# Attention in a two-block kernel: the three value pairs of a head in one burst behind its six score tiles, the sums of a head pair in the second head's burst

## What is computed

```
def _attend_dense(q, k, v):
    s = jnp.einsum('bqhd,bkhd->bhqk', q, k, preferred_element_type=jnp.float32) * (QK_DIM ** -0.5)
    pr = jax.nn.softmax(s, axis=-1).astype(v.dtype)
    return jnp.einsum('bhqk,bkhd->bqhd', pr, v)

def _merge(p, attn_o, four_o, w_o_attn, w_fourier, w_out):
    ga = jax.nn.sigmoid(p[..., OFF_GA:OFF_GB])
    gb = jax.nn.sigmoid(p[..., OFF_GB:N_IN])
    return (ga * (attn_o @ w_o_attn) + gb * (four_o @ w_fourier)) @ w_out
```

## Time and profile before

| what | us |
|---|---|
| median of 3 runs (1334.64 to 1336.63) | 1335.6 |
| span of the profiled execution | 1332.2 |
| TensorE busy in it | 1313.8 (99%) |
| the eight heads, from the first score product of head 0 to the first product of attn_o | 89.4 (278.26 to 367.64) |

### The profile page before, as it was taken

One profiled execution on the slowest core, in us unless ns is written; L12 is line 12 of the kernel. 1 busy time (PEld: TensorE's weight loads), 2 busy tenths in 40 slices (PEclk: granted clock), 3 DMA queues, 4 the chain that ended last, 5 costly groups with the idle time before them and its releaser, 6 DMA issues.

```text
span 1332.2 us, 15820 instructions
## 1 busy us (share of the span) xinstructions
PE 1313.8 (99%) x6366; PEld 966.9 (73%) x6366; DVE 690.1 (52%) x1261; ACT 461.6 (35%) x618; POOL 433.8 (33%) x136
## 2 busy tenths in 40 slices
PE   8999999999999899999999999999999999999998
PEld 6789888865587834343457788888888888888887
DVE  2465987757783733343356656612562551551553
ACT  4335223345621221121135571433341431431431
POOL 3143244247612000000015333444245344444440
PEclk9999999999999899999999999999999999999999
DMA  9521198201025799999983122222132223123101
GB/s 378 214 96 64 58 356 336 103 1 64 32 96 189 294 375 421 421 421 420 421 367 127 63 80 110 96 95 95 63 126 98 93 95 118 71 94 126 64 1 64
DMA packets 34501, 226.70 MB, mean 170 GB/s; under 512 B 4064, under 2 KB 4704, under 8 KB 8448
## 3 DMA queue, kind: packets, MB, share of 16 engines
q1 hardware_dynamic: 32992, 218.93, 42.9%
q0 software_dynamic: 1152, 4.19, 0.8%
q10 hardware_dynamic: 288, 2.62, 0.5%
HBM read 221.53 MB, written 4.19 MB: 169 GB/s over the span
## 4 chain that ended last, share of the span: by engine, by line
PE 94%; DVE 3%; DMA 1%; ACT 1%; SPq 0%; issue 0%; DVEq 0%; ACTq 0%
PE psum L961 24%; PE psum L963 23%; PE psum L962 23%; PE psum L1465 13%; DMA mod_in<-in_stream 1%; PE psum L1273 1%; PE psum L1239 1%; PE psum L1450 1%; PE psum L1453 1%; PE psum L1008 1%; PE psum L1537 1%; PE psum L1425 1%; PE psum L1674 1%; DVE rs L2381 1%; PE psum L1013 0%; DVE work L2512 0%
## 5 line engine op out<-in xcount | busy, mean ns | idle before, releaser
L895 POOL TENSOR_TENSOR w_lo<-raw,w_hi 128x2048 fp32r<-128x2048 f32 x79 | 365.3, 4627 | 589.9 <-ACT w_hi L1704 589.9
L961 PE MATMUL psum<-b_hi,w_hi 128*128 128x512 f32 x608 | 238.1, 392 | 0.1
L963 PE MATMUL psum<-b_hi,w_lo 128*128 128x512 f32 x608 | 236.7, 389 | 0.0
L962 PE MATMUL psum<-b_lo,w_hi 128*128 128x512 f32 x608 | 236.6, 389 | 0.0
L1704 ACT ACTIVATE w_hi<-raw 128x2048 fp32r<-128x2048 f32 x80 | 152.6, 1907 | 145.4 <-PE psum L963 101.9
L961 PEld LDWEIGHTS psum<-b_hi,w_hi 128*128 128x128 f32 x608 | 114.1, 188 | 30.6 <-issue 5.7
L963 PEld LDWEIGHTS psum<-b_hi,w_lo 128*128 128x128 f32 x608 | 114.1, 188 | 23.9
L962 PEld LDWEIGHTS psum<-b_lo,w_hi 128*128 128x128 f32 x608 | 114.2, 188 | 23.4
L1465 PE MATMUL psum<-ex_ring,xe 128*64 128x512 f32 x488 | 108.8, 595 | 0.9 <-ACT xe L1929 0.9
L2429 DVE TENSOR_TENSOR x<-psum,x 128x512 f32<-128x512 f32 x40 | 27.4, 691 | 124.3 <-PE psum L963 124.3
L961 PE MATMUL psum<-h_hi,w_hi 128*128 128x512 f32 (+1 forms) x208 | 84.7, 407 | 1.3 <-POOL w_lo L878 1.3
(11 more groups left out here) (419 smaller groups left out, 2290.9 us busy)
## 6 DMA issues: line engine op xcount, KB each, us to landing
raw<-in_stream SPq DMA_DIRECT2D x97, 1024.0 KB, 4.8
ex_ring<-in_stream SPq DMA_DIRECT2D x89, 1024.0 KB, 17.7
mod_in<-in_stream SPq DMA_DIRECT2D x8, 1024.0 KB, 21.0
ex_last<-in_stream SPq DMA_DIRECT2D x7, 1024.0 KB
x<-in_x SPq DMA_DIRECT2D x4, 512.0 KB, 6.0
x<-in_x ACTq DMA_DIRECT2D x1, 2048.0 KB, 7.4
xt<-h2t SPq DMA_DIRECT2D x8, 256.0 KB, 11.7
out<-y_out SPq DMA_DIRECT2D x8, 256.0 KB, 3.3
```

Source lines behind the costliest of these rows:

```text
L895: nc.gpsimd.tensor_tensor(w_lo[:, slot, :], raw[:, raw_slot, :], w_hi[:, slot, :].bitcast(F32), ALU.subtract).then_inc(w_lo_done, 1)
L961: mm(o, w[0], x[0], start=start, stop=False)
L962: mm(o, w[0], x[1], start=False, stop=False)
L963: return mm(o, w[1], x[0], start=False, stop=stop)
```

## The change

In the plan, `sums` moves from the third score tile of an even head to the end of an odd head, from bank 5 to bank 1, and stands ahead of `mx_row`. On TensorE the third value pair moves from behind score tile 2 of the next head to the end of its own head's burst, and `sums` of a head pair follows directly behind the value pairs of the second head. On ScalarE the output of a head is taken behind exponential 1 instead of 2, and `rs` behind `max_row` at the end of an odd head. VectorE and GpSimd keep their order.

```diff
@@ make_plan
             p.add("sT", h, k, by="act", bank=k % 3)
-            if k == 2 and h >= 2 and h % 2 == 0:
-                p.add("sums", h // 2 - 1, by="act", bank=5)
             if k >= 2 and h + 1 < H:
                 max_pair(h + 1, k - 2)
+        if h % 2 == 1:
+            p.add("sums", h // 2, by="act", bank=1)
         if h + 1 < H:
             p.add("mx_row", h + 1, by="act", bank=0)
         if h + 2 < H:
             head_t(h + 2)
-    p.add("sums", H // 2 - 1, by="act", bank=5)
@@ TensorE
-                    if k == 2 and h >= 1:
-                        pv_pair(h - 1, KT - 2)
-                        if h % 2 == 0:
-                            prob_sums(h // 2 - 1)
                     if k >= 2 and h + 1 < H:
                         max_pair(h + 1, k - 2)
-                pv_pair(h, 0)
-                pv_pair(h, 2)
+                for k in range(0, KT, 2):
+                    pv_pair(h, k)
+                if h % 2 == 1:
+                    prob_sums(h // 2)
                 if h + 1 < H:
                     max_row(h + 1)
                 if h + 2 < H:
                     head_t(h + 2)
-            pv_pair(H - 1, KT - 2)
-            prob_sums(H // 2 - 1)
@@ ScalarE
-                    if k == 2 and h >= 1:
+                    if k == 1 and h >= 1:
                         output(h - 1)
-                        if h % 2 == 0:
-                            output_sums(h // 2 - 1)
...
                 if h + 1 < H:
                     max_row(h + 1)
+                    if h % 2 == 1:
+                        output_sums(h // 2)
             output(H - 1)
             output_sums(H // 2 - 1)
```

## The result

| what | before | after |
|---|---|---|
| median in a joint measurement (8 runs each), us | 1335.8 | 1339.9 |
| ratio after to before, 95% interval | | 1.0032 [1.0021, 1.0044] |
| span of the profiled execution, us | 1332.2 | 1338.1 |
| to the first score product of head 0 | 278.26 | 279.29 |
| from there to the first attn_o product | 89.38 | 94.06 |

The changed kernel is slower by 0.32%, about 4.3 us. The prediction was 1338.7 us, slower, with 1336.6 to 1340.4 as its range. In the profiled execution the eight heads take 4.68 us more, where +3.15 was forecast. The 1.03 us before the first head arise in the first 47 us, where TensorE's listed waits for the input transfer `mod_in` (1.3 us for 0.8) and for ScalarE's squares of the input (2.3 for 0.7) are longer.

What follows compares the result with a forecast made beforehand. TensorE was taken as the bound, each head's reductions going at VectorE's pace. Head differences (+0.86, +1.68, -1.16, +1.64, -1.18, +1.65, -1.18, 0) and attn_o's +0.84 gave +3.15 us: 1335.6 becomes 1338.7 us, range 1336.6 to 1340.4.

Steps and rivals of the forecast that it cites:

- longer GpSimd chain: Rival: VectorE's att_lo in head 7 hold GpSimd's additions longer, +1.8 us on top, 1340.5 us; chance 0.13.
- What the move saves: TensorE's value bursts: merging the third pair takes out 1.10 us for 0.86 put in; alone -1.7 us in all.
- seven times: The count of the merged burst's 0.24 us saving across the heads, giving -1.7 us if nothing else happened.
- The wait for GpSimd: Odd heads: sums wait for the same head's last addition, 0.5 us in head 1, 0.2 in heads 3 and 5.
- One unbroken list on VectorE: First reduction of head 2 to that of head 3 stays 11.63 us, so head 3's reductions start 3.58 behind its start.
- The swapped counter values: Heads 2, 4, 6: first score product waits until rs is copied, 1.98 us behind the maxima for 1.44; +0.54, three times.
- Could it be free?: Whether the rs wait before even heads is covered: only if the transposes covered it, and they end at 1.44 us.
- Head 7: Sums start behind GpSimd's last addition, 8.36 us after the head's start as before; the pair that leaves gains 0.
- loss of 0.09 an instruction: Head 7's GpSimd additions beside VectorE's att_lo: overlap read as costing 0.09 us each, 0.27 over three.
- Bank 1: Start of attn_o: its second tile waits for the copy of rs to free the bank, +0.84 us.
- The covers: Rival: value pairs and transposes cover the new waits, leaving only the switching saved, -1.7 us, 1333.9 us; chance 0.07.
- three kinds of wait: Rival: one kind is covered, the attn_o wait or two of three rs waits; some +2.2 us, 1337.8 us; chance 0.20.

Runs made afterwards that it cites:

- e7: The changed kernel itself measured and profiled once more, nothing altered; ratio to the kernel before 1.0028, heads 94.07 us.
- e4: Kernel before with only the third value pair moved into its own head's burst, sums left in the next even head; ratio to before 1.000.
- e5: Changed kernel with the third value pair put back behind score tile 2 of the next head, so only the sums move; ratio to before 1.0041.
- e3: Changed kernel with the last sums put back in bank 5 instead of bank 1; ratio to the kernel before 1.0026.
- g5: Changed kernel with VectorE's reciprocals of pairs 0 and 1 moved to the end of heads 3 and 5, products a head later; ratio to before 1.0018.
- e6: Changed kernel with TensorE summing the last two probs of head 7, one GpSimd addition fewer; ratio to the kernel before 1.0019.
- e1: Changed kernel with a counter of its own for the copy of the sums, so first score products needn't wait for rs; ratio to before 1.0046.
- g3: e4 with VectorE's reciprocals alone moved to the end of heads 3 and 5, pair products left, second rs buffer; ratio to before 0.9991.
- g1: e4 with VectorE's reciprocal and pair product of pairs 0 and 1 moved to the end of heads 3 and 5; ratio to before 1.0060.
- g2: g1 with TensorE also summing the last two probs of head 7, as in e6; ratio to the kernel before 1.0053.
- g4: g3 with TensorE also summing the last two probs of head 7, as in e6; 1332.96 against 1336.34 us before, ratio 0.9973.

## Why the prediction came out as it did

Direction, mechanism and most terms held; the sum was 1.53 us short in the profiled heads (+4.68 for +3.15). Both medians (1339.9, and 1339.8 in e7) lie in the range, but partly by luck: its upper part was made for a longer GpSimd chain, of which only 0.25 us came, and the clock fall that filled it wasn't foreseen.

| term | predicted | measured |
|---|---|---|
| head 0 | 10.54 | 10.54 |
| heads 1; 2; 4; 6 | 12.58; 10.62; 10.62; 10.54 | 12.60; 10.59; 10.55; 10.51 |
| head 3 | 13.28 | 14.46 |
| head 5 | 13.28 | 13.53 |
| head 7, to the sums | 8.36 | 8.61 |
| sums to attn_o | 1.87 + 0.84 | 2.67 |

- **What the move saves.** The six-pass burst and the 1.10 for 0.86 are right by heads 1 (10.90 to 10.61 in e4) and 2. But "seven times" was wrong as a statement of what is there to gain: e4, which has the move and neither wait, gained it once. The even heads of after are short because pair and sums left together, and the odd ones paid for it (e5).
- **The wait for GpSimd.** 0.41 in head 1, predicted 0.5. In heads 3 and 5 predicted 0.2, measured none. TensorE came later there, by the next point.
- **"One unbroken list on VectorE", 11.63.** This step failed. From head 2's first reduction to head 3's it took 11.84 (304.97 to 316.81). The list wasn't unbroken before either: between head 2's eight reductions VectorE waited 0.45 us for TensorE (the longest 0.32), and now it waits 0.68 (twice 0.29). The reductions of head 3 therefore started 3.79 behind the head's start, not 3.58, and those of head 5 3.82. That is most of the +0.25 of head 5 and as much of head 3.
- **The clock.** The rest of head 3, 0.93 us, has no term in the prediction at all. All head windows of the kernel before read 1.00, and I asked of each added wait what it costs, not what it may do to the clock. e3, the same heads without the fall, has 13.51 in head 3. With g5 (no `k_lo` wait, no fall) the cause is narrowed to the longer wait, though not proved: see below. After and e7 have the fall in head 3, e6 with the same list up to there has it in head 5, e3 has none, so it differs from one execution to the next, and the medians don't show how often it comes.
- **The swapped counter values.** 1.99 from the row of maxima to the next head (300.44 to 302.43), predicted 1.98. The size was right and its meaning half wrong. "Could it be free?" was asked of the transposes only. e1 shows that the wait stood in for one that the place of `rs` on ScalarE brings anyway, so the swap costs nearly nothing (0.07 over heads 1 and 2). The price belongs to copying `rs` between `max_row` and the splits.
- **Head 7.** The pair that left gained nothing, as predicted, and became TensorE's wait of 1.38. But the sums came 0.25 later. GpSimd's and VectorE's instructions there, after (for the earlier trace rows):

```profile
365.89 4.65 POOL L917 TENSOR_TENSOR psum_odd<-psum_odd,probs 128x512 f32<-128x512 f32 x3
```

```profile
366.60 4.49 DVE L2070 TENSOR_TENSOR att_lo<-att,att_hi 128x512 fp32r<-128x512 f32 x3 [0.95 <-ACT att_hi L1709]
```

  Three additions took 4.65 us for 4.39. e4, which doesn't move the sums, has the same 8.62 us to the sums, so it isn't the sums' move. Taken one by one, an addition lasts 1.28 or 1.29 us alone and 1.53 or 1.54 where a VectorE product of two SBUF inputs (`att_lo`, in g3 also the pair product) is still going on at its start. In the kernel before one of the three was held so, after the change two, in e4 two, in g3 all three (4.90, sums at 8.89): 0.25 us each. `att_lo` starts 1.61 us behind the first of these three in the kernel before and 0.71 after, so it meets one addition more. So the "loss of 0.09 an instruction" was 0.27 spread over three where one alone had it. This is the direction of the rival with the longer GpSimd chain, at a seventh of its size (0.25 of 1.8). VectorE paid far more: an `att_lo` takes 0.68 alone and up to 1.76 here, since each that meets an addition ends 0.55 behind the addition's end.
- **Bank 1.** 0.84 predicted, 0.80 by e3.

The other rivals fall. The covers did not hold (head 1 stays at 12.6), and none of the three kinds of wait was absent.

## What to carry to other kernels

When a stretch of the bounding engine gets shorter, follow every other engine's list into the next stretch: here VectorE's 3.4-us reciprocal, already just on the path, took back what the merged burst saved, and moving that one instruction took 1.97 us off the heads (g3's 88.29 for e4's 90.26). Move a reader to where its inputs have long been there: sums over GpSimd's additions belong in the next head, with its scores as cover (e4's heads take 90.26 us, after's 94.06, of which 0.93 is the clock fall). Before moving a two-input product on VectorE, look which long GpSimd instruction stands beside the new place.

## What the hardware showed

- **In the heads, the granted clock fell only near a wait of 1.0 us or more.** In seven profiles (after, e7, e1, e3, e6, g1, g2) TensorE waited 1.0 us or more for VectorE, twice each, in heads 3 and 5 or 4 and 6. Seven times the clock went to 0.50 (1.2 GHz), 2.1 us behind the end of that wait in after, for 3.4 us in after and 10.2 in g1; in g1's head 6 it fell 0.5 us before the wait's end. Seven times it didn't, twice in e3, whose list in heads 0 to 6 is that of after. In none of the six kernels whose waits in heads 0 to 6 stayed at 0.9 or less (before, e4, e5, g3, g4, g5) did it fall, nor behind head 7's waits of 1.3 to 1.6 us. So the fall goes with the wait but doesn't always follow it, and no experiment here varied the wait alone. Behind 1.0-us waits it cost 0.93 us (3.4 us at 0.50) or 2.6 (6.8 us), as much as the wait itself or more.
- **Elsewhere it fell in every profile, once without a wait.** In all thirteen profiles, the kernel before among them, the clock is at 0.50 once between 84 and 92 us, for 3.4 or 6.8 us. No wait over 0.25 us stands in the 14 us ahead of it; in the kernel before TensorE made 32 products of one column each there, back to back and counted as busy, from 81.4 to 85.1 us. It is also at 0.50 between 442 and 477 us, in one or two stretches of 6.8 to 13.7 us together; there waits of up to 1.8 us stand near it. In the kernel before this stretch runs from 457.06 to 463.89 us (same columns as above, the clock third from the end):

```profile
456.00:460.00 4.00, 3.96 (x21) 3.63 (x21) 2.63 (x13) 0.00 (x0) 1.09 (x1) 0.63 0.35 134
460.00:466.00 6.00, 6.00 (x40) 6.00 (x39) 5.55 (x24) 0.25 (x1) 1.60 (x2) 0.68 0.69 209
```

- **The time of an execution goes with its mean granted clock.** Up to 436 us all thirteen profiles agree within 0.07 us, counted from `attn_o`'s start; over the next 50 us, with these stretches, they part by up to 2.1. In the 26 runs of the kernel before that were made beside e7, the fastest took 1332.6 us at a mean clock of 0.997, the slowest 1338.2 at 0.992.
- **A VectorE product of two SBUF inputs was held for 2.9 us** by one GpSimd subtraction of 4.57 us (g1), and 1.1 us (1.75 for 0.69) beside 1.3-us additions (g3). GpSimd's additions lost 0.25 us each to it. The reciprocal, of one input, took its usual 3.33 us with its last 1.5 beside such a subtraction.
- **Spread of the start.** The time to the first score product, the same instructions everywhere, varied by 2.8 us between profiles, as much as most edits here are worth. It goes with the stretch between 84 and 92 us: in the four profiles where that took 3.4 us the first head begins at 278.26 to 279.29, in the nine where it took 6.8 at 280.16 to 281.06.
